# First layer's MLP tail of a hybrid encoder: another order on five engines, other places for squares and residual, weights of the next units in tiles of their own

## What is computed

```
def rms_norm(x, g):
    xf = x.astype(jnp.float32)
    y = xf * lax.rsqrt(jnp.mean(xf * xf, axis=-1, keepdims=True) + EPS)
    return (y * g.astype(jnp.float32)).astype(x.dtype)

def conv_gated_mlp(h, w_up, conv_w, conv_b, w_down):
    u = h @ w_up
    ...
    for i in range(CONV_W):
        c = c + up[:, i:i + s] * conv_w[i]
    gate, val = jnp.split(c, 2, axis=-1)
    return (jax.nn.gelu(gate, approximate=True) * val) @ w_down

for l in range(DEPTH):
    h = rms_norm(x, norm_mix_pre[l])
    z = h @ w_in[l]
    ...
    x = x + rms_norm(mix, norm_mix_post[l])
    h = rms_norm(x, norm_ffn_pre[l])
    x = x + rms_norm(conv_gated_mlp(h, ...), norm_ffn_post[l])
```

## Time and profile before

| | us |
|---|---|
| median of 3 runs | 3843.44 |
| profiled execution | 3842.05 |
| its span (first to last instruction) | 3840.3 |
| PE busy | 3672.4 (96%) |
| DVE / ACT / POOL busy | 1859.2 / 1567.3 / 1156.3 |
| 1871 to 2005: PE / DVE / ACT / POOL busy, of 134.0 | 83.8 / 68.2 / 53.8 / 50.2 |

### The profile page before, as it was taken

How to read it: one execution, slowest core, us unless ns; L and a number is a source line. 1 busy time by engine, 2 the same in 40 slices (tenths; PEclk the granted TensorE clock), 3 DMA queues, 4 the chain that set the end, 5 groups by cost and what they waited for, 6 DMA issues and landing times. The chain is left out here.

```text
span 3840.3 us, 49855 instructions
## 1 busy us (share of the span) xinstructions
PE 3672.4 (96%) x18289; PEld 3032.5 (79%) x18289; DVE 1859.2 (48%) x2933; ACT 1567.3 (41%) x2503; POOL 1156.3 (30%) x840
## 2 busy tenths in 40 slices
PE   7899999989999999999859999999899999999997
PEld 5687777768788888888647777777687888888886
DVE  5123877964443333444431248689545333334435
ACT  3332877984411122221333338779743122221113
POOL 2223444433411222221242334534334222122123
PEclk9999999999999999999979999999999999999998
DMA  4322221103111111111223122211131111111112
GB/s 141 122 66 83 69 66 32 39 23 120 61 39 33 44 38 38 38 38 33 99 65 120 59 80 71 62 28 36 51 114 45 34 43 38 38 38 38 33 44 110
DMA packets 202443, 227.43 MB, mean 59 GB/s; under 512 B 14751, under 2 KB 162757, under 8 KB 202245
## 3 DMA queue, kind: packets, MB, share of 16 engines
q1 hardware_dynamic: 202285, 225.37, 19.5%
HBM read 173.86 MB, written 51.48 MB: 59 GB/s over the span
## 5 line engine op out<-in xcount | busy, mean ns | idle before, releaser
L237 PE MATMUL ps<-hh,wh 128*128 128x512 f32 (+1 forms) x2784 | 1012.7, 364 | 82.1 <-POOL hl L2350 36.3
L238 PE MATMUL ps<-hl,wh 128*128 128x512 f32 (+1 forms) x2784 | 993.6, 357 | 0.0
L239 PE MATMUL ps<-hh,wl 128*128 128x512 f32 (+1 forms) x2784 | 992.1, 356 | 0.0
L2319 POOL TENSOR_TENSOR wl<-raw,wh 128x1024 fp32r<-128x1024 f32 x128 | 306.4, 2400 | 1282.7 <-ACT wh L2169 1282.7
L237 PEld LDWEIGHTS ps<-hh,wh 128*128 128x128 f32 x2784 | 531.9, 191 | 167.0 <-issue 72.3
L238 PEld LDWEIGHTS ps<-hl,wh 128*128 128x128 f32 x2784 | 531.9, 191 | 81.0 <-issue 7.4
L239 PEld LDWEIGHTS ps<-hh,wl 128*128 128x128 f32 x2784 | 531.1, 191 | 75.7
L2374 DVE SCALAR_TENSOR_TENSOR cb<-ps,params,cb 128x1023 f32<-128x1023 f32 (+1 forms) x172 | 143.9, 878 | 870.4 <-ACT cb L2178 870.4
L1469 DVE TENSOR_TENSOR pl<-ps,ph 128x512 fp32r<-128x512 f32 (+1 forms) x576 | 375.3, 652 | 54.8 <-ACT ps L1314 54.4
L1423 DVE TENSOR_REDUCE mx<-ps 128x1 f32<-128x512 f32 x480 | 330.7, 689 | 141.8 <-PE ps L1228 82.8
L1313 ACT ACTIVATE ph<-ps 128x512 fp32r<-128x512 f32 (+1 forms) x576 | 329.6, 572 | 158.7 <-PE ps L1194 153.4
(11 more groups left out here) (231 smaller groups left out, 5531.5 us busy)
## 6 DMA issues: line engine op xcount, KB each, us to landing
raw<-in_w_up SPq DMA_DIRECT2D x88, 512.0 KB, 3.9
heads<-stage SPq DMA_DIRECT2D x38, 640.0 KB, 3.5
raw<-in_w_down SPq DMA_DIRECT2D x44, 512.0 KB, 3.7
rq<-heads SPq DMA_DIRECT2D x56, 320.0 KB, 4.8
raw<-in_w_in SPq DMA_DIRECT2D x32, 512.0 KB, 5.0
rk<-heads SPq DMA_DIRECT2D x32, 320.0 KB, 4.7
raw<-in_w_out SPq DMA_DIRECT2D x16, 512.0 KB, 4.4
residual<-my SPq DMA_DIRECT2D x32, 256.0 KB, 2.1
```

Of the source, the lines that this page charges most:

```text
L237: pe.matmul(out, wh, xh, start=(k == 0), stop=False)
L238: pe.matmul(out, wh, xl, start=False, stop=False)
L239: last = pe.matmul(out, wl, xh, start=False, stop=(k == len(pairs) - 1))
L2319: pool.tensor_tensor(c.wl[slot][:], c.raw[parity][:], c.wh[slot][:].bitcast(F32), ALU.subtract).then_inc(w_lo, units)
```

## The change

It concerns the tail of the first layer and what hands over weights to the phases behind it.

- DVE's order is written anew (`middle_tail`): a block's eight scalings stand together instead of alternating with additions of items and squares; the three last square additions of block 0 come before the additions of items 8 to 10; the low parts of a block (chunks 6 and 7) stand together; chunks 2, 4, 6 of the last block get their residual on DVE.
- The new squares lie in `c.squares`, at the place of `hh` (the normed input that the up units have read), one place per chunk; block 0 uses block 1's columns. The residual lies in `x_all`, at the place of `hl`. Its three loads stand behind the weights of units 0 and 1 on SP and start when the last up unit has been read.
- The freed place in the convolution's buffers takes `next_hi`, `next_lo` (weights of units 0 and 1) and two tiles `acc_pair` instead of one `acc_next`.
- Weights of units 2 and 3 are split in the tail, into `wh[0]`, `wh[1]` (and for the first layer at the end of `split_normed`, after the units that read these tiles); `latent_projections` no longer splits them.
- PE waits for one chunk's low part at a time in unit 0 and does chunks 0 to 3 of it between items 19 and 22; the new sums of a block stand elsewhere; items 14 to 23 go to other banks.
- The copy of the next layer's parameters moves from DVE to ACT's end.

```
-    c.acc_next = nc.alloc_sbuf_tensor_at("acc_next", [P, 512], F32, offset=h_at + (2 * KC - 1) * chunk + 4 * 512)
+    c.squares = nc.alloc_sbuf_tensor_at("squares", [P, KC, T], F32, offset=h_at)
...
-    c.x_long = take("x_long", [P, KC, 512])
-    c.x_short = take("x_short", [P, KC, 256])
-    c.x_sq = [take(f"x_sq{i}", [P, 512]) for i in range(3)]
+    c.next_hi = [take(f"next_hi{i}", [P, KC, P], F32R) for i in range(2)]
+    c.next_lo = [take(f"next_lo{i}", [P, KC, P], F32R) for i in range(2)]
+    c.acc_pair = [take(f"acc_pair{i}", [P, 512]) for i in range(2)]
...
@@ split_normed, ends of ACT and POOL @@
+                for i in range(2):
+                    act.wait_ge(next_arrived[i], 16)
+                    act.wait_ge(unit_done, 5 + i)
+                    act.activation(c.wh[i][:], c.raw[i][:], ACT.Copy).then_inc(w_hi, 1)
...
+                for i in range(2):
+                    pool.wait_ge(w_hi, 3 + i)
+                    pool.tensor_tensor(c.wl[i][:], c.raw[i][:], c.wh[i][:].bitcast(F32), ALU.subtract).then_inc(w_lo, 1)
...
@@ latent_projections @@
-                split_hi(act, c, 2, raw_arrived, w_used, w_hi, ready=4, done=2)
...
-                    if n == 0:
-                        split_hi(act, c, 3, raw_arrived, w_used, w_hi, ready=4, done=2)
...
-                for n in (2, 3):
-                    split_lo(pool, c, n, w_hi, w_lo, ready=2)
...
@@ gated_mlp, banks @@
+                                             [0, 1, 2, 3, 4, 5, 1, 2] + [4, 5, 1, 2, 4, 5, 1, 2])
+    SHORT_ADDS_ON_DVE = (2, 4, 6)
+    LOWS_ON_POOL = 6
...
@@ gated_mlp, SP @@
-                    sp.wait_ge(act_lo, FF_PAIRS)
-                    sp.wait_ge(act_lo1, 3 * FF_PAIRS)
-                    load_x(0)
-                    load_x(2)
                     load(NEXT, 0, w_in_chunk(c, L + 1, 0))
                     load(NEXT + 1, 1, w_in_chunk(c, L + 1, P))
-                    store(0)
-                    load_x(1)
+                    sp.wait_ge(w_used, first(FF_PAIRS) - 2)
+                    for b, (t0, w) in enumerate(BLOCKS):
+                        sp.dma_start(c.x_all[:, :, t0:t0 + w], c.s_x[:, :, t0:t0 + w]).then_inc(x_in[b], 16)
                     load(NEXT + 2, 0, w_in_chunk(c, L + 1, 2 * P))
                     load(NEXT + 3, 1, w_in_chunk(c, L + 1, 3 * P))
-                    store(1)
-                    store(2)
...
@@ gated_mlp, PE @@
+                    for k in chunks:
+                        if m == 0 and k < LOWS_ON_POOL:
+                            pe.wait_ge(lo_pool, LOWS_ON_POOL * b + k + 1)
+                        elif m == 0:
+                            pe.wait_ge(lo_dve, (KC - LOWS_ON_POOL) * b + k - LOWS_ON_POOL + 1)
...
+                    last_items(18, 20)
+                    unit(0, 0, range(3))
+                    last_item(20)
+                    unit(0, 0, range(3, 4))
+                    last_item(21)
+                    new_part_sums(1, 0, 4)
...
+                    sums(2)
+                    unit(0, 0, range(4, KC))
+                    unit(1, 0, range(KC))
+                    unit(0, 1, range(6))
+                    new_part_sums(2, 0, 4)
+                    unit(0, 1, range(6, KC))
+                    new_part_sums(2, 4, KC)
+                    unit(1, 1, range(KC))
+                    unit(0, 2, range(KC))
+                    unit(1, 2, range(KC))
...
@@ gated_mlp, ACT @@
-                        if KC * b + k >= 3:
-                            act.wait_ge(new_part, KC * b + k - 2)
-                        act.activation(c.x_sq[(KC * b + k) % 3][:, 0:w], tail_y(b, k), ACT.Square).then_inc(new_squared, 1)
+                        wait_added(act, b, k)
+                        act.activation(new_square(b, k), tail_y(b, k), ACT.Square).then_inc(new_squared, 1)
...
+                    squares(4, KC)
+                    roots(0)
+                    squares(KC, KC + 3)
+                    new_squares(0, range(4))
+                    squares(KC + 3, KC + 5)
+                    for k in range(4, KC):
+                        new_squares(0, (k,))
+                        if k < KC - 1:
+                            square(KC + 1 + k)
+                    new_roots(0)
```

More of the change, by code:

```diff
@@ L2068, in sums @@
                         pe.wait_ge(scaled, KC * b)
[L2069 removed]
+                    pe.matmul(bank(c, R1, w), c.ones[:], tail_acc(b), start=True, stop=True).then_inc(summed, 1)
                 def new_sum(b, k):
@@ L2312, in _ @@
+                    square(19)
+                    new_squares(1, (5,))
+                    square(20)
+                    new_squares(1, (6,))
+                    squares(21, 23)
+                    new_squares(1, (7,))
+                    square(23)
+                    new_roots(1)
+                    roots(2)
+                    high(1, range(KC))
+                    split_next(3, c.wh[1])
+                    new_squares(2, range(KC))
                     new_roots(2)
                     high(2, range(KC))
+                    act.wait_ge(scaled, 3 * KC)
```

339 lines of the change are left out of this document (188 added, 151 removed).

## The result

The median of the changed kernel is 3800.81 us (4 runs, 3799.45 to 3802.01), beside 3844.28 us for the kernel before (4 runs here): a ratio of 0.9887, 95% interval 0.9876 to 0.9899. It is 43.5 us faster. The forecast was 3805 in a range of 3794 to 3822, so the direction came out as predicted and the time 4 us lower. The two profiled executions took 3842.05 and 3800.70 us, with spans of 3840.3 and 3798.9.

A forecast was written before the change was run, and what follows sets the result against it. It took the tail's once-per-block chain through all engines, with PE waiting for POOL's `hl`, as the bound. Tail -39.7, next phase -1.1, first layer +2.3 made -38.5: 3842.05 to 3803.5, plus 1.4 for the median, 3805; range 3794 to 3822.

The forecast's parts named there:

- Step 1: Block 0's first sum and root: sum at 1885.8, first scaling at 1888.2 instead of 1890.7, or 1889.2 at half clock.
- Step 2: Block 0's eight scalings together on DVE end at 1893.7; POOL's additions, 1.25 us each, are slower and end at 1898.9.
- Step 3: Block 0's second sum and root: DVE's second scaling at 1904.1 against 1919.08 before, 15 us earlier.
- Step 4: POOL's list with waits by chunk: low parts start at 1905.4, block 1's at 1928.8; the list runs to 1944.
- Step 5: PE's remaining units over blocks 1 and 2: tail ends at 1958.5 against 1998.2, 39.7 us less.
- rival (c): PE alone bounds the rest after 1904.5: 43.4 us of work, end at 1948.2, 49 us less in all, 3794; chance 0.08.
- Step 6: Start of the projections, with units 2 and 3 split earlier: first layer +2.3 us, second layer -1.1.
- What was cost at nothing: Parameter copy on ACT, the residual's loads and the stores on SP were all taken as hidden, adding no time.
- (a): DVE's two-input operations are held until POOL pauses; DVE's last low parts of block 1 end 4 us later, 3809; chance 0.15.
- (b): PE's clock stays at 1.2 GHz through the interleaved stretch, 1889 to 1923: 18 us more, 3823; chance 0.12.
- (d): Second scalings wait for slow stores: at 16.5 us a store, 33 us later in all; from 21, slower; chance 0.03.
- (e): The tail is no shorter because something unseen ends it: +1.2 us, 3845, no change; chance 0.03.

The follow-up runs named there:

- run with the sums behind: Changed kernel with block 0's new sums of chunks 4 to 7 put behind items 15, 18, 19 and 20 on PE; 3804.74 us, ratio 0.9895.
- the ring's run: Changed kernel with the new squares in three places in turn, each waiting for the sum three before, as in the kernel before; 3800.05 us, ratio 0.9886.

## Why the prediction was right, step by step

Times here are on the clock before (2.32 taken off).

- **Step 1** gave the first scaling for 1888.2; it came at 1888.71 (1890.70 before). The sum itself is not 0.4 earlier, as I had it, but stands at 1886.23 (1886.19 before); the gain of 2 us is the sum's 1.13 us in place of 2.07, and 1.1 less from its end to the scaling, since ACT goes straight to the root.
- **Step 2** was right: eight scalings in a row of 5.36, and POOL's additions as the slower of the two (9.97). They end at 1899.6 for 1898.9.
- **Step 3** gave 15 us for the second scaling (1904.1); it is 13.8 (1905.30). The run with the sums behind shows that each of these microseconds counts at the end of the tail.
- **Step 4** had POOL's list: first low part 1905.4 (1906.8 measured), block 1's 1928.8 (1928.95), the last short one ended 1951.8 (1950.13). Its pauses came where they were expected. What the sharing costs POOL was off both ways: two low parts of DVE pushed it by 0.47 (2.82 for a weight of 2.35) where the sum had 1.4, and the five short additions beside DVE's took 4.76 where it had 3.9. That the list still ends within 1.7 us is in part luck. What the waits by chunk are worth is shown by two comparisons, 16.5 us of tail on the kernel before and 7.8 on the changed one.
- **Step 5 failed in its sizes.** It put the end at 1958.5, and it is 1954.8 (1957.12 less 2.32). Of the 3.7 us, 1.6 is the clock term: I charged two spells at 1.2 GHz on the new tail, and the granted clock is 1.00 in each of the rows above that lie between 1880 and 1950. The other 2.1 lies where PE comes through block 1. The sum let PE wait for DVE's last two low parts there until about 1942, and had PE through the two chunks and the four sums behind them at 1945.3. The low parts were done at 1940.85 (1943.17), PE had by then done the first of the two chunks, and was through at 1943.24 (1945.56). From there the 11.6 us that the sum has to the end are right (11.56). So the lists of POOL and DVE are not behind PE, as the sum had it, but level with it: in this kernel PE's own work decides all but 0.1 us after 1929.92, and where POOL's list is longer, that decides. From the second scaling to the end it takes 49.5 us, 3.2 of them waits (1.5, 1.5 and 0.2), so 46.3 of work. That is rival (c)'s mechanism in part, with its own size off: it had 43.4 of work and no waits. Where PE's other 2.9 us of work come from stays open.
- **Step 6**: +2.3 and -1.1 were predicted, the waits gave +2.13 (8.05 less 5.92) and -1.11 from table load to matmul. Not foreseen is that the phases behind both handovers are longer, from PE's first matmul to ACT's next table load by 0.4 (68.69 against 68.26) and 0.8 us (69.59 against 68.83). The first is less than the ten kernels with one and the same first layer differ among themselves (68.53 to 70.16). Behind the second, PE runs at 1.2 GHz for 4.8 us where it did so for 4.0 in the kernel before; how much of the 0.8 that makes is open.
- **What was cost at nothing.** The parameter copy lies on ACT under PE's work, the residual's loads cost nothing (POOL's first addition waits for DVE and not for them), nor does the squares' place (the ring's run). For the stores the prediction named the condition, that the loads of units 2 and 3 ahead of them wait for POOL's first weight and that this is done early. It is, and where a run broke it, it cost 8.5 us; that the weights' own tiles are what keeps it was not said.
- **Rivals.** (a) didn't occur in this kernel (1.26, 0.72 and 0.86 for the three additions) and did in the one with all low parts on POOL; (b), half clock, did not occur; (d), late stores, occurred only where a waiting load was put in front of them; (e) fell.

The sum of the errors: tail and start of the next phase -44.86 in place of -40.8, the first layer's projections start 1.65 late in place of 2.3, and some 1.8 us given back elsewhere that no step had.

## What to carry to other kernels

Where PE waits for a block, let it wait for the first chunk that it needs, and then look at what makes that first chunk late: the waits alone gave 16.5 us of tail here, the rest of the change, which brings the roots forward, 35.4 without them, and both together 43.75. When a load is put into an in-order DMA queue, ask what it waits for and what stands behind it; two loads ahead of four stores cost 8.5 us. A chain of scalings should hold nothing that waits on a third engine (3.5 us here). And a small gain in front of a new phase is to be read behind the phase's start: here 0.9 us more or 1.2 less was gone there.

## What the runs showed of the hardware

- A DVE operation with both inputs in SBUF beside POOL mostly gets in after the rest of POOL's current instruction: 1.26 us for an addition of 0.41, and 4.49 for two low parts, in which POOL's weight operation took 2.82 instead of 2.35. This agrees with the Trainium skill ("SBUF — State Buffer", "Who interferes with whom"), by which whoever comes first has the shared ports for a whole instruction. The whole-instruction rule alone doesn't cover the rest: one addition was held 9.59 us, past the ends of six low parts and two additions of POOL, and in the kernel before the copy was held 3.54. Why it gets in between two of POOL's instructions in one case and not in another stayed open; no run tells it apart.
- In the second layer PE's clock was back at 2.4 GHz 98.2 to 98.4 us after the last convolution in seven runs, whether PE started the phase 92.3 or 94.4 us after it. The spell at 1.2 GHz, 6.1 to 3.9 us, took back what was won or lost at the start. The length of the wait alone doesn't tell the spell: in the first layer the same wait of 8.05 was followed by 3.55 to 5.64 us of it.
- ACT's table load of 1.28 us at the start of a phase whose table is already there could be left out, and nothing loaded it later.
